# A mixture-of-experts stage on one core: first layer in column quarters, a weight ring of 14 slots, overflow loads issued by ScalarE

## What is computed

```
def _moe(x, wr_g, br_g, wr_e, br_e, w_gate, w_up, w_down):
        ...
        lg = (xs @ wr_g).astype(f32) + br_g
        pg = jax.nn.softmax(lg, axis=-1)
        ptop, gsel = lax.top_k(pg, 1)
        ...
        lv, esel = lax.top_k(le, MOE_TOPK)
        we = jax.nn.softmax(lv, axis=-1) * ptop
        ...
        hg = jnp.einsum('sd,edh->seh', xs, w_gate)
        hu = jnp.einsum('sd,edh->seh', xs, w_up)
        h = jax.nn.silu(hg) * hu * gate[..., None].astype(xs.dtype)
        return jnp.einsum('seh,ehd->sd', h, w_down)
```

## Time and profile before

| | |
|---|---|
| median of three runs | 1963.24 us (1962.75 to 1963.44) |
| device time of the profiled execution | 1966.96 us |
| span of the profiled execution | 1965.2 us |
| mean granted clock of TensorE | 0.952 |
| TensorE busy, matmuls / weight loads | 1773.5 us (90%) / 1366.5 us (70%) |
| VectorE, ScalarE, GpSimd busy | 949.5, 757.8, 100.9 us |
| chain that ended last: PE, DMA, DVE, ACT | 75%, 11%, 8%, 4% |
| chain's share of ring<-wall | 10% |
| experts' stage, first matmul to end of last scatter | 511.9 to 816.6 us |

### The profile page before, as it was taken

The page is one execution under the profiler, slowest core; times in us unless marked ns, Lnnn a source line. Parts: engine busy times, 40 slices in busy tenths (PEclk is TensorE's granted clock), DMA queues, the critical chain, the costliest instruction groups (busy, mean ns, idle before and its releaser), DMA issues.

```text
span 1965.2 us, 32818 instructions
## 1 busy us (share of the span) xinstructions
PE 1773.5 (90%) x12838; PEld 1366.5 (70%) x12838; DVE 949.5 (48%) x1741; ACT 757.8 (39%) x1399; POOL 100.9 (5%) x158
## 2 busy tenths in 40 slices
PE   6888779987799999899999899999998799989997
PEld 6775657776444444487778588788876686789997
DVE  4742543377622211427344655435535454568684
ACT  5331323453122111423564533323335334555454
POOL 0010000004000000100000200000002000010000
PEclk8998889997899999999999899999998899989999
DMA  5598546766288889722101123222321230135552
GB/s 222 174 238 304 173 174 226 262 209 182 108 330 317 332 314 344 271 78 77 39 1 44 54 92 101 86 97 86 103 87 58 86 108 1 48 123 185 182 181 77
DMA packets 84850, 303.43 MB, mean 154 GB/s; under 512 B 10144, under 2 KB 12192, under 8 KB 84576
## 3 DMA queue, kind: packets, MB, share of 16 engines
q1 hardware_dynamic: 80640, 290.49, 42.8%
q0 software_dynamic: 2736, 7.35, 1.6%
q10 hardware_dynamic: 1328, 3.55, 0.5%
HBM read 347.22 MB, written 3.15 MB: 178 GB/s over the span
## 4 chain that ended last, share of the span: by engine, by line
PE 75%; DMA 11%; DVE 8%; ACT 4%; issue 2%; SPq 0%; ACTq 0%; DVEq 0%
PE bank L888 47%; PE bank L833 17%; DMA ring<-wall 10%; PE bank L1351 3%; PE bank L912 2%; PE bank L1389 2%; PE bank L1364 2%; PE bank L1374 2%; DVE w_lo L2028 1%; ACT w_hi L1581 1%; DVE BIG L2640 1%; DMA con<-consts 1%; PE bank L1411 0%; ACT XC L1650 0%; ACT BIG L1642 0%
## 5 line engine op out<-in xcount | busy, mean ns | idle before, releaser
L888 PE MATMUL bank<-BIG_f32r,w_hi 128*128 128x256 f32 (+1 forms) x2208 | 552.6, 339 | 23.6 <-DVE BIG_f32r L2043 15.6
L2028 DVE TENSOR_TENSOR w_lo<-ring,w_hi 128x1024 fp32r<-128x1024 f32 x260 | 322.6, 1250 | 352.5 <-ACT w_hi L1581 351.2
L888 PEld LDWEIGHTS bank<-BIG_f32r,w_hi 128*128 128x128 f32 x2208 | 382.8, 192 | 73.5 <-issue 25.5
L888 PE MATMUL bank<-BIG_f32r,w_lo 128*128 128x256 f32 (+1 forms) x1136 | 387.6, 341 | 0.0
L1581 ACT ACTIVATE w_hi<-ring 128x1024 fp32r<-128x1024 f32 x260 | 271.5, 1053 | 246.5 <-PE bank L888 157.1
L888 PE MATMUL bank<-AR_f32r,w_hi 128*128 128x256 f32 (+1 forms) x1066 | 268.7, 331 | 16.7 <-issue 9.4
L888 PEld LDWEIGHTS bank<-BIG_f32r,w_lo 128*128 128x128 f32 x1136 | 217.2, 191 | 25.4 <-issue 0.2
L888 PEld LDWEIGHTS bank<-AR_f32r,w_hi 128*128 128x128 f32 x1066 | 186.1, 193 | 37.6 <-issue 9.9
L888 PE MATMUL bank<-AR_f32r,w_lo 128*128 128x256 f32 (+1 forms) x448 | 147.5, 329 | 0.0
L888 PE MATMUL bank<-lnst_f32r,w_hi 128*128 128x256 f32 x318 | 101.2, 318 | 36.6 <-DVE w_lo L2028 33.4
L888 PE MATMUL bank<-XC_f32r,w_lo 128*128 128x256 f32 x424 | 127.6, 301 | 0.0
(11 more groups left out here) (357 smaller groups left out, 2294.4 us busy)
## 6 DMA issues: line engine op xcount, KB each, us to landing
ring<-wall SPq DMA_DIRECT2D x546, 512.0 KB, 4.6
w_extra<-wall SPq DMA_DIRECT2D x96, 512.0 KB
BIG<-t_rows POOLq DMA_DIRECT2D x16, 128.0 KB, 13.4
AR<-na_rows POOLq DMA_DIRECT2D x32, 64.0 KB, 7.4
con<-consts ACTq DMA_DIRECT2D x1, 1810.0 KB, 12.0
na_rows<-rpb_pad POOLq DMA_DIRECT2D x1, 1792.0 KB, 32.5
XC<-xin ACTq DMA_DIRECT2D x1, 1024.0 KB, 6.4
XC<-ctxin POOLq DMA_DIRECT2D x1, 1024.0 KB, 6.4
```

The source lines that it names most:

```text
L888: ins = nc.tensor.matmul(o, l, r, start=start and n == 0, stop=stop and n == 2, **kw)
L2028: V.tensor_tensor(w_lo[:, i % SPLIT_RING, :], ring[:, t % RING, :], w_hi[:, i % SPLIT_RING, :].bitcast(F32), ALU.subtract).then_inc(w_spli ...
```

## The change

- `moe_up` runs 32 matmuls of 128 columns in place of 8 of 512. For each k, four column groups take a quarter of the 512 columns each, with the same `Xb` slice as weights. The sum over k is then complete in each group, and bank 0 is used in 128 columns.
- `moe_fold` becomes `moe_turn`, with one transpose of 128 x 128 in place of four matmuls. ScalarE's copy to `m_h` has 128 columns in place of 512.
- The ring has 14 slots in the first 140 tiles of the stage (8 of them in `BIG`, called far slots), 10 in the next 30, and 6 in the last 16 (`moe_slot`). The first far load waits for the norm ahead (`ln_out`).
- `load_extra` moves from SyncE's stream to ScalarE's, behind its copy of the selection in block n = `held_until` + 1. The first loads of `w_extra` (expert 0) stay with SyncE.
- The order of blocks is 0, 1, 2, overflow 0, 3, 4, overflow 1, ..., 29, 30, overflow 14, 31.
- The context's pieces run at n = 38 to 45 and 39 to 46, and VectorE first waits for TensorE to give up the last tile in far slots 4 to 7.
- The four clearing matmuls go; the first scatter starts its banks itself. The constants `zeros` and `fold` go.

```
+CTX_FROM = 38
...
-        if e % 2 and e // 2 < EXTRA:
-            order.append(EXPERTS + e // 2)
+        if e and e % 2 == 0:
+            order.append(EXPERTS + e // 2 - 1)
...
+FAR = 8
...
+def moe_slot(i, moe0):
+
+    if i < 140:
+        j = i % (RING + FAR)
+        return (moe0 + j) % RING if j < RING else j
+    if i < 170:
+        j = (i - 140) % (RING + FAR // 2)
+        return (moe0 + 170 + j) % RING if j < RING else j
+    return (moe0 + i) % RING
...
+        def slot(t):
+            q = slot_at[t]
+            return ring[:, q, :] if q < RING else BIG[:, (q - RING) * TILE:(q - RING + 1) * TILE]
...
+                        if t == moe0 + RING:
+                            sp.wait_ge(w_used, last_split_use)
+                            for e in range(6):
+                                sp.dma_start(w_extra[:, e, :], wall[moe0 + e]).then_inc(extra_ready[e], 16)
+                            sp.wait_ge(sem("ln_out"), KC)
+                    before = earlier[t]
+                    if before is not None and before in split_at:
+                        sp.wait_ge(w_split, split_at[before] + 1)
+                    elif before is not None:
+                        sp.wait_ge(w_free, whole_at[before] + 1)
+                    sp.dma_start(slot(t), src).then_inc(w_ready[slot_at[t]], 16)
...
-                    g, c0 = k % 4, (k % 2) * 512
-                    ins = nc.tensor.matmul(ps[0][32 * g:32 * g + 32, :], Xb[:, n % 2, k, :], w[:, c0:c0 + 512],
-                                           start=k < 4, stop=k >= 4, tile_position=(0, 32 * g))
...
+                    for g in range(4):
+                        c0 = (k % 2) * 512 + g * P
+                        ins = nc.tensor.matmul(ps[0][32 * g:32 * g + 32, 0:P], Xb[:, n % 2, k, :], w[:, c0:c0 + P],
+                                               start=k == 0, stop=k == KC - 1, tile_position=(0, 32 * g))
...
-                for c in range(4):
-                    ins = nc.tensor.matmul(ps[1][:, c * SLOTS:(c + 1) * SLOTS], m_h[:, c * P:(c + 1) * P], c_("fold"),
-                                           start=True, stop=True)
-                ins.then_inc(sem("moe_tr"), 1)
+                nc.tensor.transpose(ps[1][:, 0:P], m_h, ident).then_inc(sem("moe_tr"), 1)
...
-                                               m_selT[r, n % 3, :], start=False, stop=n == MOE_BLOCKS - 1 and c == 1,
+                                               m_selT[r, n % 3, :], start=n == 0 and c == 0,
...
-            for bb in range(4):
-                mm(ps[4 + bb][:, :], c_("zeros"), con[:, 0:512], True, False, skip_group_check=True)
...
+            held_until = [0] + [moe_order.index(EXPERTS + e) for e in range(EXTRA - 1)]
+            extra_after = {n + 1: e for e, n in enumerate(held_until)}
+
+            def load_extra(e):
+
+                if e == 0:
+                    act.wait_ge(sem("moe_table"), 1)
+                act.wait_ge(sem("moe_y"), held_until[e] + 1)
+                expert = act.value_load(i_experts[0:1, e:e + 1], min_val=0, max_val=EXPERTS - 1)
+                needed = act.value_load(i_needed[0:1, e:e + 1], min_val=0, max_val=1)
+                for q in range(6):
+                    act.dma_start(w_extra[:, q, :], wall[expert * 6 + (moe0 + q)], cond=needed,
+                                  bounds_check="skip_entire_dma").then_inc(extra_ready[q], 16)
...
-                f(m_h, ps[0], ACT.Copy).then_inc(sem("moe_h"), 1)
+                f(m_h, ps[0][:, 0:P], ACT.Copy).then_inc(sem("moe_h"), 1)
...
+                if n in extra_after:
+                    load_extra(extra_after[n])
...
+                if n == CTX_FROM + 1:
+                    dve.wait_ge(w_free, whole_at[last_in_far] + 1)
+                if CTX_FROM + 1 <= n < CTX_FROM + 1 + KC:
+                    context_low(n - CTX_FROM - 1)
```

More of the change, by code:

```diff
@@ L226, in build @@
     moe1 = moe0 + stage_tiles["moe"]
+    slot_at, earlier, landed, held_by, times = {}, {}, {}, {}, [0] * (RING + FAR)
+    for t in range(n_tiles):
+        q = moe_slot(t - moe0, moe0) if moe0 <= t < moe1 else t % RING
+        slot_at[t], earlier[t] = q, held_by.get(q)
+        held_by[q] = t
+        times[q] += 1
+        landed[t] = 16 * times[q]
+    last_in_far = max(t for t in range(moe0, moe1) if slot_at[t] >= RING + FAR // 2)
     def run_end(t):
@@ L412, in build @@
         Xb = aM.take(2, KC, SLOTS)
-        m_h = aM.take(512)
+        m_h = aM.take(P)
         m_sg = aM.take(2, SLOTS)
@@ L694, in _ @@
             stream = moe_stream()
-            extra_from = {(max(moe_order[i - 2], 1), 5): i for i, b in enumerate(moe_order) if b >= EXPERTS}
-            def load_extra(i):
-                n = moe_order[i] - EXPERTS
-                if n == 0:
-                    sp.wait_ge(w_used, last_split_use)
-                    for q in range(6):
-                        sp.dma_start(w_extra[:, q, :], wall[moe0 + q]).then_inc(extra_ready[q], 16)
-                    sp.wait_ge(sem("moe_table"), 1)
-                sp.wait_ge(sem("moe_y"), moe_order.index(EXPERTS + n - 1 if n else 0) + 1)
-                expert = sp.value_load(i_experts[0:1, n:n + 1], min_val=0, max_val=EXPERTS - 1)
-                needed = sp.value_load(i_needed[0:1, n:n + 1], min_val=0, max_val=1)
-                for q in range(6):
-                    sp.dma_start(w_extra[:, q, :], wall[expert * 6 + (moe0 + q)], cond=needed,
-                                 bounds_check="skip_entire_dma").then_inc(extra_ready[q], 16)
             while t < n_tiles:
@@ L736, in _ @@
                         src = wall[moe0 + 6 * b + q]
-                    sp.wait_ge(freed, place[t - RING] + 1)
-                    sp.dma_start(ring[:, t % RING, :], src).then_inc(w_ready[t % RING], 16)
-                    if in_moe and (b, q) in extra_from:
-                        load_extra(extra_from[b, q])
+                        if t == moe0 + RING:
[9 more added lines that the diff above has]
+                    sp.dma_start(slot(t), src).then_inc(w_ready[slot_at[t]], 16)
                     t += 1
@@ L868, in tile @@
                     return w_hi[:, split_at[t] % SPLIT_RING, :], w_lo[:, split_at[t] % SPLIT_RING, :]
-                return ring[:, t % RING, :]
+                return slot(t)
             def hold(stage, n0, n):
@@ L876, in hold @@
                     if q < n - 1:
-                        pe.wait_ge(w_ready[t % RING], 16 * (t // RING + 1))
-                    ws.append(ring[:, t % RING, :])
+                        landed_in(pe, t)
+                    ws.append(slot(t))
                 state["tile"], state["held"] = first[stage] + n0 + n - 1, n
@@ L882, in held_last @@
             def held_last():
-                pe.wait_ge(w_ready[state["tile"] % RING], 16 * (state["tile"] // RING + 1))
+                landed_in(pe, state["tile"])
             def split_sum(o, a, b_, start, stop, done=None, **kw):
@@ L2838, in shape_constants @@
     put("pick", pick.reshape(P, 4))
-    put("fold", np.tile(np.eye(32), (4, 1)))
     return c
```

33 lines of the change are left out of this document (17 added, 16 removed).

## The result

The changed kernel takes 1909.32 us, the median of four runs (1908.92 to 1910.02), against 1963.34 us (1962.75 to 1964.20) for the kernel before in the same series. The ratio is 0.9731, with a 95% interval of 0.9717 to 0.9745. The forecast was 1896 us with a range of 1876 to 1922: 54 us were won where 67 were expected. The profiled execution took 1909.41 us with a span of 1907.6, so it stands at its median; the one of before was 3.6 us above its own.

The account below looks back on a forecast made before the run. The experts' stage was taken as bound by DMA transfers with gaps behind overflow loads. With 172 tiles taking 234 us it would end at 750 instead of 816.6, 67 us less: 1963.2 - 67 = 1896 us, range 1876 to 1922.

Parts of the forecast that it names:

- Bound of the kernel before: Experts' stage, 511.9 to 816.6 us: DMA transfers plus a 3 us gap behind each of 15 overflow loads make 299 us.
- two causes named for the gap: SyncE stands still 3.4 us in `load_extra`; six slots hold only 7.9 us of transfers at 400 GB/s.
- First layer in quarters, one transpose: TensorE's blocks: first layer 1.83 us; replacing the fold saves 0.75 us, so a block takes 4.30 instead of 5.05.
- The rival of open weight loads: First layer 3.5 us, each weight load exposed; block 6.0, TensorE ends at about 792, total 1938 us; chance 0.05.
- the slower one: Rival: four column groups run one after another, first layer 6.8 us, block 9.3, total 2097 us; chance 0.04.
- ScalarE's queue: Overflow loads there stall TensorE 15 times 1.0 us, plus 2; rival: 2.5 to 4 each, 1901 to 1922 us, chance 0.12.
- Transfers decide: Stage's ring: 172 tiles at 385 GB/s, 1.362 us each, 234 us; last tile at 747, stage ends 750; forecast chance 0.51.
- The rival with 401 to 430 GB/s: Faster transfers, so TensorE's path decides and ends between 727 and 742: 1874 to 1889 us; chance 0.18.
- The ceiling of 358 GB/s: Rival: transfers asked without pause run at 359 GB/s, 251 us, stage ends at 767, total 1914 us; chance 0.08.
- Loads flow from 513: Start of stage: first slot comes free at 512.3 us, so ring loads run from 513 and not from 527.
- In the last 46 tiles TensorE waits for data anyway: End of stage: with 10 and then 6 slots TensorE waits for data anyway.
- The granted clock should stay 1.00: TensorE in the stage: clock is 1.00 (2.4 GHz) in every window before and should stay so with fewer gaps.

Follow-up runs that it names:

- thin tiles: Changed kernel, but 105 of the stage's 172 ring tiles load only 256 of their 1024 columns: 1888.31 us, ratio 0.9611.
- late loads on SyncE: Changed kernel with overflow loads back in SyncE's stream, issued behind the last tile of the block just before the overflow block: 1909.84 us, ratio 0.9725.
- six under way: Changed kernel, 14 slots kept, but SyncE allows at most 6 tile loads of the stage in flight at once: 1905.83 us, ratio 0.9712.
- table in pieces: Changed kernel with VectorE's overflow-slot table cut in two, behind the products of blocks 0 and 1, instead of all ahead of block 0: 1902.60 us.
- table in pieces, six under way: Changed kernel with VectorE's overflow-slot table in two parts and at most 6 tile loads in flight: 1901.93 us, ratio 0.9685.
- late loads, table in pieces: Changed kernel with overflow loads in SyncE's stream behind the block before, and VectorE's table in two parts behind blocks 0 and 1: 1915.56 us.
- halves: Changed kernel with the old first layer (8 matmuls of 512 columns), four fold matmuls and 512-column copy, all else as changed: 1930.70 us, ratio 0.9856.
- three under way: Changed kernel with at most 3 tile loads of the stage in flight at once: 1969.40 us, ratio 1.0036.

## Why the prediction was right, and where it was off

**Bound of the kernel before: right.** Transfers with gaps. The quarters alone gave nothing (304.0 us of stage), though at a clock of 0.89, the loads on ScalarE with what goes along gave 19 us with six slots, and the eight slots another 33. So of the two causes named for the gap, the six slots weighed more.

**First layer in quarters, one transpose: right.** Forecast 1.83 us a layer and 4.30 a block, measured 1.86 and 4.30. The rival of open weight loads is out. So is the slower one: 64 records in 1.86 us are 29 ns each. (The 792 of the first of these rivals left out the 3.8 us behind the blocks and ScalarE's stalls, which the forecast's own path has; its 1938 us were too low.) The Trainium skill's rule ("TensorE: Matmul & The Clock Gate", What overlaps and what doesn't), by which loads on the same rows are not hidden, would have made 3.5 us of it; the trace disagrees for four column groups side by side.

**ScalarE's queue: right in size, and in weight for the middle only.** 13 stalls of 0.9 us, 11.2 us in all, against 15 of 1.0 and 2 us for the context pieces, and in the run with thin tiles 15 of 14.6 us. Without them (late loads on SyncE) the middle of the stage stays as long, and the last 46 tiles come 7.7 us faster, by the table below. That the whole time stayed the same is luck.

**Transfers decide: right in the middle, and the rate was mis-sized.** Forecast 385 GB/s, measured 403 for 150 us: 1.301 us a tile in place of 1.362, which over 172 tiles should have ended the stage 10.5 us earlier, near 740. The rival with 401 to 430 GB/s had the rate, but said TensorE's path would then decide, with 1874 to 1889 us. With four tiles, 5.20 us of transfers, to a block, and 4.30 us of TensorE's with its stalls on top, the two were level. The traces show when each ring tile landed, so the stage can be cut there. After the 14 tiles that are loaded ahead of it (12 in the two runs with the late loads), 172 follow: in us, the time from its start to the landing of the 13th of them, for the next 113 (as long as there are 14 slots), for the last 46, and the rest:

| run | start | next 113 | last 46 | rest | stage |
|---|---|---|---|---|---|
| changed kernel | 29.4 | 149.4 | 69.3 | 4.2 | 252.2 |
| six under way | 29.0 | 149.5 | 69.6 | 4.4 | 252.6 |
| table in pieces | 25.1 | 148.5 | 70.0 | 2.6 | 246.2 |
| table in pieces, six under way | 24.5 | 150.2 | 67.9 | 2.8 | 245.4 |
| late loads on SyncE | 38.6 | 148.6 | 61.6 | 5.2 | 254.0 |
| late loads, table in pieces | 35.5 | 155.7 | 63.9 | 7.9 | 263.0 |
| thin tiles | 28.8 | 131.8 | 70.6 | 3.8 | 235.1 |
| halves | 32.2 | 163.0 | 77.8 | 3.6 | 276.5 |

With full tiles and quarters the 113 take 148.5 to 150.2 us with TensorE's stalls or without them (155.7 where the clock fell; with the halves TensorE decides), and only fewer bytes make them faster. That shows the transfers as what decides there. The ceiling of 358 GB/s in the Trainium skill ("DMA: Bandwidth & Descriptors", Where 436 GB/s comes from) isn't seen here: with one core at work, 403 were held for 150 us.

**"Loads flow from 513": wrong by 5 us.** From 510 to 535 us 6.7 MB moved, where 385 GB/s from 513 would have been 8.5. The slots were shut because TensorE stood: it waited 3.8 us for VectorE (the 3.0 us for GpSimd lie ahead of the first layer at 507.69, where the forecast had them) and then ran at half clock. VectorE's overflow table is work that the kernel before had too. There TensorE was done with block 1's first layer at 517.74 (515.82 + 1.92), and the product behind the table (517.77 to 517.99) was there before ScalarE's copy of that layer, which TensorE needs too; now it is done at 512.46, and the product comes at 516.11. The forecast asked what ScalarE and GpSimd had to do at the start, and not VectorE. The run with the table in two pieces shows this term: 6 us of stage.

**"In the last 46 tiles TensorE waits for data anyway": wrong.** When the ring shrinks from 14 slots to 10 and 6, SyncE must let the tiles ahead be used up before it may issue again. From 730 to 745 us the engines moved 227 GB/s, which at 403 is 6.6 us of transfers lost, and from 685 to 730 us 388, another 1.7. The first load that has to wait for the tile six places ahead is issued at 735.47, 9.5 us behind the one before it; its slot's tile had landed at 729.41, but TensorE came to it late, held up by a stall of 1.92 us and the clock behind it. So TensorE was not waiting for data: tiles lay ready in front of it. Where it was waiting, in the run with the late loads, the same shrinking cost little: its last 46 tiles took 61.6 us, and at 403 GB/s they would take 59.8. The forecast's sentence would have held for a TensorE without stalls. A change of the shrinking alone was not tried, so how the 9.5 us of the changed kernel divide between it and TensorE's stalls is open.

**"The granted clock should stay 1.00": wrong.** Four stretches at 0.50, behind idle times of 1.5 to 3.8 us, cost 1.3 to 1.7 us each. Three of the four follow a stall for instructions, which the forecast didn't know of. I had counted columns and loads of the quarters, and not that each of them is an instruction to be fetched.

**The sum.** From the forecast's end at 750: -10.5 for the rate, +5 for the start and +8 for the shrinking make 753. Measured is 759.9. The rest lies in the last 15 us, where 329 GB/s were moved (2.8 us of transfers short), in what follows the last tile (it landed at 755.7, and TensorE took 4.2 us behind it where 2.7 were forecast), and in what I can't place, 3 us. The 3.6 us by which the profiled execution of before lay above its median widen the distance in the whole time: the profiles differ by 57.6 us, the medians by 54.0.

## What to carry to other kernels

When a stage is limited by two sides that wait for each other, price each part of a change against the other parts and not alone: here the quarters were worth 0 or 24 us and the long ring 0 or 33, depending on what stood beside them (and partly on TensorE's clock). After lengthening a ring, look at every wait placed in the loader's stream at a fixed position: it is reached earlier by as many slots, and one such wait, reached too early at 15 places, cost 50 us. Where a ring is to shrink again, ask whether its consumer lags behind: the last 46 tiles took 69.3 us with a TensorE that lagged and 61.6 with one that waited for them. And when a run comes out at the same time as another, cut both into stretches before calling a term free: here 9 us lost at the start hid 8 won at the end.

## What the hardware did that I had not expected

- TensorE seems to run out of instructions: that is inferred from the packets' times, no row says it. The packets of 16 KB share the DMA engines with the data. At a DMA share of 1.02 (403 GB/s) 23 packets in 150 us went with 12 stalls of 11.0 us, and at a share of 0.50 26 packets went with none. A stall ended 2.3 to 2.8 us after a packet's beginning, with 14 tiles under way as with 6. In the middle of the stage it cost nothing, because the transfers were as slow.
- Four idle times of TensorE in the changed kernel, of 1.52 to 3.79 us, were each followed by a stretch at a granted clock of 0.50 (1.2 GHz), in which layers took 1.3 to 1.9 times as long. It doesn't follow each time: a wait of 1.82 us that ended at 742.88 left the clock at 1.00, and so did three stalls of 1.52 to 1.58 us in the run with the table in pieces.
- One queue of 512 KB loads moved 300 GB/s with three under way and 401 with six. With 14 nothing more came, only the landing went from 7.6 to 10.2 us.
- Satisfied waits on TensorE cost about 33 ns each: 71 of them were 2.4 us on average.
